# Where a query normalisation stands in a fused attention and expert kernel: splitting it around the attention loop, halving small products, and moving one row store behind weight loads

## The reference, cut to what matters

```python
z = _rms(x, g_mix) @ w_in                      # split into q_lat, c_kv, kr_raw, dq, dk, dv, ga, gb
q = (_rms(q_lat, g_q_lat) @ w_uq).reshape(b, s, 8, 64 + 32)
q_nope = _rms(q[..., :64], g_mla_qn)
q_rope = _rope(_rms(q[..., 64:], g_mla_qr), pos)
ckv = _rms(c_kv, g_kv_lat)
k_nope = _rms((ckv_all @ w_uk).reshape(b, -1, 8, 64), g_mla_kn)
v_a = (ckv_all @ w_uv).reshape(b, -1, 8, 128)
...                                            # o_a: softmax attention over q, k, v_a; o_b: differential attention
h = x + (sigmoid(ga) * o_a + sigmoid(gb) * o_b) @ w_out
h = h + _hier_moe(_rms(h, g_ffn), ...)         # 32 experts, two per token
h = h + sigmoid(_rms(h, g_ple) @ w_ple_gate) * (pe @ w_ple_proj)
```

## Time and profile before

| what | value |
|---|---|
| median of three executions | 1020.78 us (1017.55 to 1024.54) |
| profiled execution | 1024.93 us |
| its span, first to last instruction | 1023.1 us |
| mean granted clock of PE | 0.953 of full |
| busy time PE, DVE, ACT, POOL | 895.9, 471.2, 358.1, 202.6 us |
| bytes read and written in HBM | 163.92 MB, 21.64 MB |

### The profile page before, as it was taken

One profiled execution on the slowest core, in us unless ns is written; L12 is line 12 of the kernel. 1 busy time (PEld: TensorE's weight loads), 2 busy tenths in 40 slices (PEclk: granted clock), 3 DMA queues, 4 the chain that ended last, 5 costly groups with the idle time before them and its releaser, 6 DMA issues.

```text
span 1023.1 us, 12617 instructions
## 1 busy us (share of the span) xinstructions
PE 895.9 (88%) x4341; PEld 608.5 (59%) x4341; DVE 471.2 (46%) x1130; ACT 358.1 (35%) x835; POOL 202.6 (20%) x305
## 2 busy tenths in 40 slices
PE   6899999999999699999769997927998777878898
PEld 6787878787878476555546775823333222323686
DVE  3463363637474599567657624271111111104562
ACT  3632443434242598632425523201111111104331
POOL 1231221303030144665400010001110101010100
PEclk9999999999999899999779998957999999999999
DMA  7244242322220511011211158677999999995511
GB/s 227 92 115 143 62 131 81 117 73 83 83 63 21 183 44 30 15 63 65 91 31 45 60 142 344 229 272 258 414 418 419 418 418 420 417 416 222 185 42 52
DMA packets 80084, 179.07 MB, mean 175 GB/s; under 512 B 16850, under 2 KB 32260, under 8 KB 80020
## 3 DMA queue, kind: packets, MB, share of 16 engines
q1 hardware_dynamic: 71556, 160.27, 43.6%
q0 software_dynamic: 7424, 17.98, 4.7%
q10 hardware_dynamic: 1040, 0.00, 0.1%
HBM read 163.92 MB, written 21.64 MB: 181 GB/s over the span
## 4 chain that ended last, share of the span: by engine, by line
PE 34%; DMA 15%; DVE 5%; SPq 2%; issue 1%; ACT 1%; DVEq 0%; ACTq 0%; POOLq 0%
DMA raw_e<-in_w_ei 12%; PE acc L662 6%; PE acc L788 5%; PE acc L1425 5%; PE acc L1528 3%; PE acc L1393 3%; PE acc L678 3%; PE acc L1489 2%; PE tp L1376 2%; DMA raw_e<-in_w_eo 2%; PE acc L760 1%; PE tp L1512 1%; DMA raw<-in_w_out 1%; PE acc L1588 1%; PE tp L651 1%
## 5 line engine op out<-in xcount | busy, mean ns | idle before, releaser
L1393 PE MATMUL acc<-whi,lhi 128*128 128x512 f32 (+2 forms) x432 | 169.4, 392 | 5.6 <-DVE wlo L1830 5.6
L1393 PE MATMUL acc<-whi,llo 128*128 128x512 f32 (+2 forms) x432 | 166.1, 385 | 0.0
L1393 PE MATMUL acc<-wlo,lhi 128*128 128x512 f32 (+2 forms) x432 | 166.1, 385 | 0.0
L662 PE MATMUL acc<-raw_e,xT 128*64 128x512 f32 x512 | 125.0, 622 | 28.6 <-DMA raw_e<-in_w_ei 27.1
L1631 ACT ACTIVATE whi<-raw,gcol 128x512 fp32r<-128x512 f32 (+2 forms) x96 | 61.5, 689 | 121.1 <-issue 115.2
L662 PEld LDWEIGHTS acc<-raw_e,xT 128*64 128x64 f32 x512 | 37.8, 141 | 110.3 <-issue 108.2
L1393 PEld LDWEIGHTS acc<-whi,lhi 128*128 128x128 f32 x432 | 81.7, 189 | 24.6 <-DVE wlo L1830 8.6
L1393 PEld LDWEIGHTS acc<-whi,llo 128*128 128x128 f32 x432 | 81.5, 189 | 16.7
L1393 PEld LDWEIGHTS acc<-wlo,lhi 128*128 128x128 f32 x432 | 81.7, 189 | 15.5
L1830 DVE SCALAR_TENSOR_TENSOR wlo<-raw,gcol,whi 128x512 fp32r<-128x512 f32 (+2 forms) x96 | 64.8, 716 | 47.2 <-ACT whi L1631 47.1
L1528 PE MATMUL acc<-vh,prT 128*128 128x128 f32 (+2 forms) x384 | 67.1, 306 | 6.2 <-DMA vh<-in_cache_v 3.2
(11 more groups left out here) (257 smaller groups left out, 1467.3 us busy)
## 6 DMA issues: line engine op xcount, KB each, us to landing
raw_e<-in_w_ei SPq DMA_DIRECT2D x128, 512.0 KB, 16.0
raw_e<-in_w_eo SPq DMA_DIRECT2D x64, 512.0 KB, 16.4
raw<-in_w_in SPq DMA_DIRECT2D x40, 512.0 KB, 3.6
raw<-in_w_out SPq DMA_DIRECT2D x8, 512.0 KB, 6.4
wp_raw<-in_w_ple_gate SPq DMA_DIRECT2D x8, 512.0 KB, 9.2
raw_e<-y_rows SPq DMA_DIRECT2D x4, 1024.0 KB, 8.4
va_rows<-raw POOLq DMA_DIRECT2D x12, 256.0 KB, 3.1
vh<-va_rows SPq DMA_DIRECT2D x8, 384.0 KB, 3.5
```

What stands on the lines that cost most here:

```text
L662: mm = pe.matmul(acc[rows, 0, :], xT[:, 2 * c + k, rows], raw_e[:, slots[2 * c + b], 512 * k:512 * k + 512], start=(c == 0 and k == 0), st ...
L1393: mm = pe.matmul(bank, x, W[w], start=(kk == 0 and x is hi and w == 0), stop=(kk == c.kt - 1 and x is lo))
```

## The change

Four edits.

1. The norms of `last_uq` are split: square and sums of tile 0 come before the attention, with the other items; tiles 1 to 4 are squared and summed one iteration earlier than before. All five normalisations come two iterations earlier (`NORM_AT` is 2, 5, 8, 11, 14). `TURN_AT` stays.
2. In the latent products tile 4 is multiplied in two halves of the columns: the 64 real rows are the stationary side (64 columns) twice, once in the left half of the array for the first half of the columns, once in the right half for the second. ACT copies the two halves out in two instructions.
3. One wait of ACT ahead of the attention goes; the same wait now stands in front of the square of tile 0.
4. On SP, two loads of expert weights and four of the gate weights come ahead of the last store of rows; the gate load that lands on the gain row, which DVE's L1964 still reads, comes behind it.

```diff
-    NORM_AT = {3 * t + 4: t for t in range(TILES)}
+    NORM_AT = {3 * t + 2: t for t in range(TILES)}
...
             for n in (14, 15, 16, 17, 21, 22):
                 fixed_tile(sp, n)
-                if n == 17:
-                    store_rows(TILES - 1)
-            for k in range(3, 8):
+            for k in range(3, 7):
                 gate_weights(k)
+            store_rows(TILES - 1)
+            gate_weights(7)
...
-                            for k in range(c.kt):
+                            wide = c.width // 2
+                            for k, b in [(k, b) for k in range(c.kt) for b in range(2)] if t == PT else ():
+                                mm = pe.matmul(acc[DEC * b:DEC * b + DEC, t, 0:wide], L[:, k, t * P:t * P + DEC],
+                                               W[:, k, c.col + wide * b:c.col + wide * b + wide],
+                                               start=(k == 0), stop=(k == c.kt - 1))
+                            for k in range(c.kt) if t != PT else ():
...
+                    elif c.kind != "gate" and t == PT:
...
+                        for b in range(2):
+                            ins = act.activation(out[:, wide * b:wide * b + wide], acc[DEC * b:DEC * b + DEC, t, 0:wide],
+                                                 ACT.Copy)
...
-                    if i - 1 in ids and i - 1 != last_uq:
-                        squares(i - 1)
+                    if i - 1 in ids:
+                        squares(i - 1, [0] if i - 1 == last_uq else None)
...
-                    if ph == "a" and n < TILES:
-                        squares(last_uq, [n])
+                    if ph == "a" and n < TILES - 1:
+                        squares(last_uq, [n + 1])
...
-            act.wait_ge(ss_done, y_norm[(last_uq, 0)])
...
-                    if i - 1 in ids and i - 1 != last_uq:
-                        sums_of(i - 1)
+                    if i - 1 in ids:
+                        sums_of(i - 1, [0] if i - 1 == last_uq else None)
...
-                    if ph == "a" and 1 <= n <= TILES:
-                        sums_of(last_uq, [n - 1])
+                    if ph == "a" and 1 <= n < TILES:
+                        sums_of(last_uq, [n])
```

More of the change, by code:

```diff
@@ L1659, in copy_out @@
                             act.activation(low_part(i), low_part(i), ACT.Sigmoid).then_inc(z_copied, 1)
+                    elif c.kind != "gate" and t == PT:
+                        if uses_zs(i):
+                            wait_slot_free(act, i, t)
+                        else:
+                            act.wait_ge(outz[t], 16 * out_count(i - 1, t))
+                        wide = c.width // 2
+                        out = zs[0:DEC, t, :] if uses_zs(i) else uv_tile(t)[0:DEC, :]
+                        for b in range(2):
+                            ins = act.activation(out[:, wide * b:wide * b + wide], acc[DEC * b:DEC * b + DEC, t, 0:wide],
+                                                 ACT.Copy)
+                        ins.then_inc(z_copied, 1)
                     elif uses_zs(i):
```

## The result

| | before | after |
|---|---|---|
| median of the runs | 1019.16 us (4 runs, 1014.84 to 1024.54) | 1004.24 us (4 runs, 1002.20 to 1005.73) |
| ratio, 95% interval | | 0.9843 [0.9813, 0.9873] |
| profiled execution: span | 1023.1 us | 1002.0 us |
| mean granted clock of TensorE over the span | 0.953 | 0.961 |

The prediction was 1007 us in a range of 999 to 1017, with 0.64 on faster by over 1%. The two profiled executions differ by 21.1 us, the medians by 14.9: the profiled execution of before, 1024.93 us, was slower than all four runs of the table, the one of after, 1003.81, lies in the middle of its own. So a difference read between the two traces is some 6 us larger as a whole than what the medians show; the experiments say in which stage.

A forecast was written before the change was run, and what follows sets the result against it. PE bounds the latent products, no engine the first half of attention "a"; time won before the experts reaches the end. 3.4 + 11.0 + 2.4 = 16.8 us off 1024.9 gives 1008.1, less 1.1 for spread: 1007, range 999 to 1017.

The forecast's parts named there:

- First term: Latent products: tile 4's passes paired on the array's two halves save 3.4 us net, bounds -1.9 to 4.5.
- 0.15 for once in and out: Latent products: price in us of changing to the 64-row shape and back, 0.73 for five items.
- Second term: Attention "a": normalisations no longer in front of copies shorten the rounds, 11.0 us saved, bounds 5.5 to 13.0.
- One round of four at 0.50: Attention "a": allowance for one round still running at granted clock 0.50, about 2 us.
- the first part gains nothing: Attention "a" up to the first copy: no gain, as first values wait about 2.04 us longer.
- part of this spread is how many rounds lose the clock: Runs differ by 7 us partly through rounds losing the clock; so 1.1 of 4.1 us was taken off.
- Third term: SP's queue: six loads moved into idle DMA time shorten the first gather, gain 2.4 us, between 0 and 2.9.
- The low clock throughout: Rival, attention "a": every round still runs at 0.50, gain 5.5 us in place of 11.0, 1012.5 us; chance 0.17.
- The halves one after the other: Rival, latent products: paired passes do not run beside each other, term -1.9 us, 1012.3 us; chance 0.08.
- The stall of the softmax: Rival, attention "a": normalisations ahead of maxima delay exponentials and values, 10.2 us lost, 1028 us; chance 0.04.
- The gather that waits anyway: Rival, SP's queue: the gather waits anyway or the queue is no shorter, 1009.4 us; chance 0.07.

The follow-up runs named there:

- the halves one after the other: Changed kernel with tile 4's two loops exchanged, all passes of the left column half before all of the right: 1006.94 us, ratio 0.9895.
- the normalisations alone: Kernel before with only the move of the normalisations, the split sums and the dropped ACT wait; products and queue as they were: 1009.70 us, ratio 0.9909.
- the late `p`: Changed kernel with SP sending the loads of `p` only after the first gather has landed: 1004.35 us, ratio 0.9860.
- the queue alone: Kernel before with only SP's order changed, four gate loads (with the two of each) ahead of the last row store: 1016.07 us, ratio 0.9976.

## Why the prediction was right, and where its terms were off

**What bounds the stages** was read rightly: PE in the products, nobody in the first half of the attention, and time won ahead of the experts reaches the end. The end of the attention comes 18.5 us earlier in the trace, the first gather 20.3, the end 21.1.

**First term, latent products, 3.4 us: 2.7.** The saving by columns was right, the price of the shape was mis-sized. "0.15 for once in and out" was taken from the scores. The products saved 3.1 us where 4.48 were counted, so five times in and out cost 1.36, 0.27 each, near the double that the bounds had held ready. The blocks themselves show half of it: 1.01 us for 8 passes of 256 columns, where 0.428 ns a column makes 0.88. The other half is in the full passes around them: those of both runs take 42.05 us in the chain, where the two runs of before, 50.49, less tile 4's 9.09 leave 41.40. ACT's two copies are as foreseen: the turns and copies between the products and the first scores take 0.3 us more. On the price the Trainium skill, "TensorEngine Tiling (Array Packing)", Key Properties, has the right sign, with its rule that a change of mode drains TensorE; the size stands only in these rows. The same section says that different tiles work independently of each other, and with the halves one after the other the blocks of 8 agree (1.02 us against 1.01), the blocks of 12 not fully (1.50 against 1.13).

**Second term, attention "a", 11.0 us: 15.9 between the two traces, 9 by the runs of this part alone.** The interval of those runs goes from 7.4 to 11.1 us, so 11.0 lies at its edge. The rounds were right: 6.6, 6.6, 6.6, 6.2 predicted, 6.2, 6.9, 6.3, 5.8 measured, 14.4 us less than before. Two allowances were not needed in this execution. "One round of four at 0.50" did not come: the clock stands at 1.00 from 499 on. That is luck. Four executions here have the change's order of normalisations: this one and the halves one after the other had no such round and took 76.6 and 76.7 us for the attention; the normalisations alone and the late `p` had one of 8.2 us each and took 78.0. Such a round costs less than the 2.0 allowed: the same round without it takes 6.8 to 6.9 us, and the whole attention is 1.4 longer.

And "the first part gains nothing" was too low, by the order itself and not by luck. The first values wait 2.1 us longer, as predicted, but the first copy stands 15.1 to 15.2 us behind the first scores in all four of those executions, where it stood 16.2 to 17.0 behind them in the three with the order of before (16.6 in the trace of the prediction): tile 1's normalisation no longer stands in front of it, and by these rows that is worth more than the longer wait costs. In the trace of after the half clock lasts from 494 to 497, where it lasted from 494 to 501. The 14.4 of the rounds and the 1.5 of the first part are the 15.9.

The other side of the difference is the kernel before: three executions of its attention took 92.4, 89.6 and 88.0 us, in the order of their clocks (0.69, 0.80, 0.84), and the sum was made from the longest. The guess that "part of this spread is how many rounds lose the clock" is borne out by these, and the single runs agree: of the 49 runs of the kernel before that stand beside the experiments, the seven with a mean clock of 0.953 or less have a median of 1022.2 us, the 17 with 0.960 or more one of 1017.0. The profiled time stood about 6 us above the median of all runs of before, not 4.1, and the 1.1 taken off for it was too little. So the forecast set out from 1023.83, 4.7 above the median of 1019.16, and took off 16.8, which is 1.9 more than the medians moved. The two errors work against each other, and the 1007 is 2.8 too high; that it is no more is in part luck.

**Third term, SP's queue, 2.4 us: 1.7 in the trace of after, 2.1 alone.** The part moved the loads into the idle time as said. The term is mis-sized by the gather's length: 4.2 us taken, 4.5 to 5.2 measured.

**The rivals.** The low clock throughout is refuted by the clock of 0.96, though in single rounds it is real. The halves one after the other are refuted by the blocks: 8 passes of 256 columns take 1.01 us, where at 0.845 ns a column one after the other they would take 1.73. The stall of the softmax didn't come, though its first step did: from 480 to 545 ACT's exponentials wait 13.9 us for maxima, 2.3 at the longest, where they waited 3.6 and 1.3. PE has no wait for exponentials among its own, so its lead was not used up. The gather that waits anyway is refuted by the queue alone.

## What to carry to other kernels

Where an engine that another waits for holds two pieces of work, the one that is waited for goes first: exchanging two calls in one iteration brought as much as moving the work two iterations ahead, with shorter waits. Price a wait of PE not by its length alone but by the clock in the rows behind it, and test that with useless work in the wait before the order is rebuilt. Before a gain is summed from one execution, see how far that execution stands from the others, and look at small loads that sit in a queue ahead of a transfer on the chain: moving eight of them was worth more than half of what the whole change was.

## What was not expected of the hardware

- 64 useless products made the kernel before faster, by 4.2 parts in a thousand, as the clock of the stretch rose from 0.69 to 0.84 up to 0.96.
- The same idle stretch (0.67 and 0.78 us busy of 2) was followed by the full clock in one execution and by half of it in another.
- A half pass of 64 columns costs the same in a run of four of its own half as in turn with the other half (1.02 and 1.01 us for 8), and 0.37 us more for 12 in runs of six.
- One small issue on SP, the load of `g_ffn`, took 3.64, 2.21, 4.17, 4.21, 2.32 and 1.55 us in six executions, on the chain each time, and 1.65 to 2.40 in five more; so the chain differs by up to 2.7 us by it alone.
